# A fourth weight sum by an accumulating transfer, with some twenty steps in another order, in a fused pair of float32 transformer blocks

## The reference

```
gu = jnp.einsum('bsd,df->bsf', hn, w_gate_up[l])
act = jax.nn.silu(gu[..., :D_FF]) * gu[..., D_FF:]
h = h + jnp.einsum('bsf,fd->bsd', act, w_down[l])
```

## Time and profile before

| what | value |
|---|---|
| median of 3 runs | 1271.92 us (1271.25 to 1272.7) |
| the profiled execution | 1271.37 us, with a span of 1269.6 us |
| TensorE busy | 1253.5 us, 99% of the span |
| VectorE busy | 1042.7 us, 82% |
| ScalarE busy | 804.0 us, 63% |
| GpSimd busy | 192.4 us, 15% |
| read from HBM | 275.24 MB, 218 GB/s over the span |

### The profile page before, as it was taken

The page is one execution under the profiler, slowest core; times in us unless marked ns, Lnnn a source line. Parts: engine busy times, 40 slices in busy tenths (PEclk is TensorE's granted clock), DMA queues, the critical chain, the costliest instruction groups (busy, mean ns, idle before and its releaser), DMA issues.

```text
span 1269.6 us, 15538 instructions
## 1 busy us (share of the span) xinstructions
PE 1253.5 (99%) x5897; PEld 1028.9 (81%) x5897; DVE 1042.7 (82%) x1035; ACT 804.0 (63%) x986; POOL 192.4 (15%) x224
## 2 busy tenths in 40 slices
PE   9999999999999999999999999999999999999998
PEld 7888878888888878788778888788888877788886
DVE  6766689999799996767899997999977568999984
ACT  6674576665576664645766664766656466766662
POOL 6142130110001100102201101111001003301100
PEclk9999999999999999999999999999999999999999
DMA  9537498997649955568979978389745535999931
GB/s 333 174 100 231 133 313 254 268 270 248 201 151 255 269 168 180 188 226 215 320 249 245 271 251 255 116 237 274 219 166 173 184 125 168 315 286 262 266 135 44
DMA packets 143002, 277.32 MB, mean 218 GB/s; under 512 B 8992, under 2 KB 39896, under 8 KB 142928
## 3 DMA queue, kind: packets, MB, share of 16 engines
q1 hardware_dynamic: 120192, 229.67, 51.6%
q0 software_dynamic: 22288, 45.54, 19.7%
q10 hardware_dynamic: 448, 1.12, 0.2%
HBM read 275.24 MB, written 1.05 MB: 218 GB/s over the span
## 4 chain that ended last, share of the span: by engine, by line
PE 77%; DVE 12%; issue 4%; ACT 3%; DMA 3%; POOL 0%; DVEq 0%; SPq 0%; ACTq 0%
PE B L2102 14%; PE B L2104 14%; PE B L2103 14%; DVE w_lo L1359 7%; PE B L2558 6%; PE B L2560 6%; PE B L2559 6%; PE T L2102 3%; PE T L2104 3%; PE T L2103 3%; DMA VD<-in_ffn_w_gu 2%; DVE VD L1378 1%; DMA Z<-in_ffn_w_gu 1%; ACT w_hi L1082 1%; ACT w_hi L768 1%
## 5 line engine op out<-in xcount | busy, mean ns | idle before, releaser
L1359 DVE TENSOR_TENSOR w_lo<-w_raw,w_hi 128x2048 fp32r<-128x2048 f32 x129 | 296.5, 2299 | 87.5 <-ACT w_hi L768 87.2
L768 ACT ACTIVATE w_hi<-w_raw 128x2048 fp32r<-128x2048 f32 x129 | 247.1, 1918 | 102.7 <-PE B L2560 60.3
L2102 PE MATMUL B<-w_hi,xt_lo 128*128 128x512 f32 x652 | 260.5, 400 | 5.1 <-DVE w_lo L1359 2.1
L2104 PE MATMUL B<-w_hi,xt_hi 128*128 128x512 f32 x652 | 254.7, 391 | 0.0
L2103 PE MATMUL B<-w_lo,xt_hi 128*128 128x512 f32 x652 | 254.0, 390 | 0.0
L2558 PE MATMUL B<-w_hi,act_lo 128*128 128x512 f32 x440 | 172.5, 392 | 0.8 <-DVE w_lo L1359 0.4
L2560 PE MATMUL B<-w_hi,act_hi 128*128 128x512 f32 x440 | 171.4, 390 | 0.0
L2559 PE MATMUL B<-w_lo,act_hi 128*128 128x512 f32 x440 | 171.3, 389 | 0.0
L2102 PEld LDWEIGHTS B<-w_hi,xt_lo 128*128 128x128 f32 x652 | 122.4, 188 | 36.1 <-issue 6.2
L2104 PEld LDWEIGHTS B<-w_hi,xt_hi 128*128 128x128 f32 x652 | 122.4, 188 | 26.4
L2103 PEld LDWEIGHTS B<-w_lo,xt_hi 128*128 128x128 f32 x652 | 122.6, 188 | 23.3
(11 more groups left out here) (330 smaller groups left out, 2110.0 us busy)
## 6 DMA issues: line engine op xcount, KB each, us to landing
w_raw<-in_ffn_w_down SPq DMA_DIRECT2D x88, 512.0 KB, 5.8
Z<-in_ffn_w_gu SPq DMA_DIRECT2D x64, 512.0 KB, 8.1
w_raw<-in_ffn_w_gu SPq DMA_DIRECT2D x48, 512.0 KB, 5.2
nat<-in_ffn_w_gu SPq DMA_DIRECT2D x32, 512.0 KB, 7.8
QT<-in_ffn_w_gu SPq DMA_DIRECT2D x32, 512.0 KB, 7.0
Z<-in_ffn_w_gu POOLq DMA_DIRECT2D x32, 512.0 KB, 8.8
w_raw<-in_conv_w_in SPq DMA_DIRECT2D x24, 512.0 KB, 4.7
w_raw<-in_w_down SPq DMA_DIRECT2D x22, 512.0 KB, 6.6
```

The lines of the kernel that those rows point to most:

```text
L768: act.activation(whi[home(u)][:, :], raw[slot][:, :], ACT.Copy).then_inc(w_hi, 1)
L1359: dve.tensor_tensor(wlo[home(u)][:, :], src, whi[home(u)][:, :].bitcast(F32), ALU.subtract).then_inc(w_lo, 1)
L2102: pe.matmul(bank[:, :], lo[:, k, x], whi[s][:, c], start=first, stop=False, skip_group_check=more)
L2104: return pe.matmul(bank[:, :], hi[:, k, x], whi[s][:, c], start=False, stop=last, skip_group_check=more)
```

## The change

The changed kernel does the same arithmetic. Square 3 joins `ADDED_T4`: GpSimd issues one more accumulating transfer in each FFN, of B21 into VD, and VectorE's sum of it is gone. Besides, steps move in the lists of TensorE, VectorE and ScalarE; no matmul is added or removed. SyncE's list stays as it is.

```diff
--- before.py
+++ after.py
@@ -62,8 +62,8 @@
 OP = {name: i for i, name in enumerate(FFN_OPS)}
 FFN_UNITS = len(FFN_OPS)
 
-SUMS = ((1, "T1"), (1, "T2"), (2, "T1"), (2, "T2"), (3, "T1"), (3, "T2"), (3, "T4"))
-ADDED_T4 = (1, 2)
+SUMS = ((1, "T1"), (1, "T2"), (2, "T1"), (2, "T2"), (3, "T1"), (3, "T2"))
+ADDED_T4 = (1, 2, 3)
 
 
 def sums_of(f):
@@ -1120,11 +1120,11 @@
 
                 weights("N1b")
                 block("P1", 0)
+                act.wait_ge(rstd, 2 * ST[stat] + 2)
+                gate_of(0, u0 + OP["N0b", 0], PAIR[0] if f else F0)
                 act.wait_ge(sx_ok, f + 1)
                 act.wait_ge(w_used, u0 + OP["N0b", 0] + 1)
                 act.activation(yhi[:, :, :], xsum, ACT.Copy).then_inc(sx_hi, 1)
-                act.wait_ge(rstd, 2 * ST[stat] + 2)
-                gate_of(0, u0 + OP["N0b", 0], PAIR[0] if f else F0)
                 block("P2", 0)
                 gate_of(1, u0 + OP["N1b", 0], GU)
                 act_out(0)
@@ -1574,10 +1574,10 @@
             split_at(6)
             head_scale(1, Z[:, :, 512:1024], FOX_H, FOX_DH)
             mem_round_lo(0)
-            split_at(7)
             dve.wait_ge(c_hi, 1)
             low = slice(64, CK)
             dve.tensor_tensor(cT[low, :], B[3][low, 0:S], cT[low, :].bitcast(F32), ALU.subtract).then_inc(c_out, 1)
+            split_at(7)
             evac(EV_IN + 2, 5, Z[:, 1, 1536:2048], PAIR[2], "h0")
             heads_out(HT_KF, KT[:, 2:4, :], G_KF)
             split_at(8)
@@ -1737,13 +1737,17 @@
                     .then_inc(dve_step, 1)
                 return steps[0]
 
-            def x_sums(total):
+            def x_sums(total, second):
 
                 dve.wait_ge(dve_step, total)
                 a11, a12 = xsum[:, 0:4, 0:P], xsum[:, 4:8, 0:P]
                 a21, a22 = xsum[:, 0:4, P:S], xsum[:, 4:8, P:S]
-                link(dve.tensor_tensor(a22, a21, a22, ALU.subtract))
-                dve.tensor_tensor(a21, a11, a21, ALU.subtract)
+                if not second:
+                    steps[0] += 1
+                    dve.tensor_tensor(a22, a21, a22, ALU.subtract).then_inc(dve_step, 1)
+                    dve.wait_ge(dve_step, steps[0])
+                    dve.tensor_tensor(a21, a11, a21, ALU.subtract)
+                    return
                 link(dve.tensor_tensor(a11, a22, a11, ALU.subtract))
                 dve.tensor_tensor(a12, a12, a11, ALU.add).then_inc(sx_ok, 1)
 
@@ -1814,11 +1818,12 @@
                     hi, lo = act_parts(d)
                     dve.tensor_tensor(lo[:, :], act_bank(d)[:, :], hi[:, :].bitcast(F32), ALU.subtract).then_inc(act_lo, 1)
 
-                x_sums(total)
+                x_sums(total, False)
                 weights("N1b")
-                block("P1", 0)
+                x_sums(total, True)
                 dve.wait_ge(rstd, 2 * ST[stat] + 2)
                 act_of(0, PAIR[0] if f else F0)
+                block("P1", 0)
                 dve.wait_ge(sx_hi, f + 1)
                 dve.tensor_tensor(ylo[:, :, :], xsum, yhi[:, :, :].bitcast(F32), ALU.subtract).then_inc(sx_lo, 1)
                 block("P2", 0)
@@ -1827,11 +1832,11 @@
                 block("P5", 0)
                 block("P6", 0)
                 block("P3", 0)
-                weight_sum("T4", f, 0)
                 block("P7", 0)
                 weights("D0")
+                weight_sum("T4", f, 0)
+                result("C22", 0)
                 block("P4", 0)
-                result("C22", 0)
                 weights("D1")
                 result("C12", 0)
                 weight_sum("T1", f, 1)
@@ -1844,12 +1849,12 @@
                     square_act(p - 1, 0)
                     square_act(p - 1, 1)
                     block("P6", p)
-                    if p not in ADDED_T4:
-                        weight_sum("T4", f, p)
                     block("P3", p)
                     block("P7", p)
                     act_out(2 * p)
                     weights("Da", p - 1)
+                    if p not in ADDED_T4:
+                        weight_sum("T4", f, p)
                     act_out(2 * p + 1)
                     block("P2", p)
                     result("C22", p)
@@ -1876,9 +1881,10 @@
                 act_out(FJ - 1)
                 if kv:
                     kv_round_lo(1)
+                if kv:
+                    kv_round_lo(2)
                 split_at(u0 + FFN_UNITS)
                 if kv:
-                    kv_round_lo(2)
                     kv_round_lo(3)
                 split_at(u0 + FFN_UNITS + 1)
 
@@ -1933,9 +1939,9 @@
             conv_gate(1)
             conv_evac(4)
             split_at(U_COUT, U_COUT + 1)
-            conv_taps(2)
             conv_lo(0)
             conv_lo(1)
+            conv_taps(2)
             conv_evac(5)
             conv_taps(3)
             conv_gate(2)
@@ -2058,8 +2064,8 @@
             combine(4)
             diff_max(11)
             o_sum(1)
+            o_norm(1)
             heads_lo(0)
-            o_norm(1)
             diff_max(12)
             evac(EV_V1, U_V1 + 1, VD[:, 1, HALF:D], PAIR[1], "h6")
             combine(5)
@@ -2547,11 +2553,11 @@
                                       not first)
                     ins.then_inc(w_used, 1)
 
-                def down_part(d, u, t, half):
+                def down_part(d, u, t, half, k0=0, k1=2):
 
                     hi, lo = act_parts(d)
                     slot = home(u)
-                    for k in range(2):
+                    for k in range(k0, k1):
                         c = slice(k * D + half * HALF, k * D + half * HALF + HALF)
                         x = slice((2 * k + t) * P, (2 * k + t) * P + P)
                         o = PAIR[half][t][:, :]
@@ -2632,22 +2638,35 @@
                 turn_act(FJ - 1, GROUPS - 1)
                 if kv:
                     kv_round(1)
-                down("Db", SQUARES - 1, (lambda: kv_round(2)) if kv else (lambda: None))
+                d, u = down_ready("Db", SQUARES - 1)
+                down_part(d, u, 0, 0)
+                down_part(d, u, 0, 1)
+                if kv:
+                    kv_round(2)
+                down_part(d, u, 1, 0)
+                d1, u1 = down_ready("DN2", 0)
+                down_part(d1, u1, 0, 0).then_inc(tok0_done, 1)
                 if kv:
                     kv_round(3)
-                d, u = down_ready("DN2", 0)
-                down_part(d, u, 0, 0).then_inc(tok0_done, 1)
-                down_part(d, u, 0, 1).then_inc(tok0_done, 1)
-                down_part(d, u, 1, 0).then_inc(tok1_half, 1)
-                if nxt:
+                down_part(d1, u1, 0, 1).then_inc(tok0_done, 1)
+                down_part(d, u, 1, 1).then_inc(w_used, 1)
+                down_part(d1, u1, 1, 0).then_inc(tok1_half, 1)
+                if f == 0:
                     for j in range(4):
                         turn(nxt, 0, j, h, h_waits(nxt))
-                down_part(d, u, 1, 1).then_inc(w_used, 1)
+                down_part(d1, u1, 1, 1, 0, 1)
+                if f and nxt:
+                    turn(nxt, 0, 0, h, h_waits(nxt))
+                    turn(nxt, 0, 1, h, h_waits(nxt))
+                down_part(d1, u1, 1, 1, 1, 2).then_inc(w_used, 1)
+                if f and nxt:
+                    turn(nxt, 0, 2, h, h_waits(nxt))
+                    turn(nxt, 0, 3, h, h_waits(nxt))
 
             ffn(0, "ffn0", h_waits("ffn0"), nxt="ffn1")
-            ffn(1, "ffn1", h_waits("ffn1"), turned=True)
-
-            first_group(U_CIN, "cin", PAIR[0], h, h_waits("cin"))
+            ffn(1, "ffn1", h_waits("ffn1"), turned=True, nxt="cin")
+
+            first_group(U_CIN, "cin", PAIR[0], h, h_waits("cin"), turned=True)
             def conv_feed(p, is_b):
 
                 if not is_b:
@@ -2696,9 +2715,9 @@
                 if k < 2:
                     conv_feed(k + 2, True)
             last_group(U_COUT + 2, PAIR[1], "ffn2")
-            ffn(2, "ffn2", h_waits("ffn2"), turned=True)
-
-            ffn(3, "ffn3", h_waits("ffn3"), kv=True)
+            ffn(2, "ffn2", h_waits("ffn2"), turned=True, nxt="ffn3")
+
+            ffn(3, "ffn3", h_waits("ffn3"), kv=True, turned=True)
 
             def q_round(j):
 
@@ -2866,18 +2885,24 @@
             pe.wait_ge(w_lo, U_O + 2)
             for k in (4, 5):
                 out_heads(1, k, 0)
+            out_heads(0, 4, 1)
             heads_pair(3)
-            for k in (4, 5):
+            out_heads(0, 5, 1)
+            out_heads(1, 4, 1)
+            pe.wait_ge(ao_lo, 4)
+            for half in range(2):
+                for k in (6, 7):
+                    out_heads(half, k, 0)
+            for k in (6, 7):
                 out_heads(0, k, 1)
-            pe.wait_ge(ao_lo, 4)
-            for t in range(TOKS):
-                for k in (6, 7):
-                    out_heads(0, k, t)
-            for k in (6, 7):
-                out_heads(1, k, 0)
-            for k in range(4, KD):
+            for k in (5, 6):
                 out_heads(1, k, 1)
```

(7 more changed lines are left out.)

## The result

The changed kernel takes 1293.12 us in the median of 5 runs (1292.91 to 1294.24), the kernel before 1271.76 (1271.25 to 1272.7) beside it: the ratio is 1.017, with a 95% interval of 1.0157 to 1.0184. It is slower, as forecast, but by 21.4 us instead of 7, outside the range. The profiled execution has a span of 1291.1 us against 1269.6.

The account below looks back on a forecast made before the run. The prediction took TensorE, 99% busy at full clock, as the bound, so only its waits could change. It set 16.0 us lost against 8.9 won, +7.1, and predicted 1279.0 us, range 1269.5 to 1285.

Parts of the forecast that it names:

- the chain in square 0: VectorE's T4 behind P7 and D0 delays ScalarE's copy of P4, then act_out(1); D1 on TensorE starts 3.0 us later.
- the sum of square 0: Five FFNs: 3.0 us lost in four, 2.5 in FFN 2, plus 0.3 each for B12's load; 16.0 us lost.
- my bound from above: B12's load in square 0, at 6.6 us or slightly more, lands at 843.9, delaying T1 by up to 1.0 us.
- T4 of square 3: Its sum goes from VectorE to a covered transfer, so P3's wait in square 3 goes; 1.9 us won.
- The x_sums in halves: At N1b, the low part comes 1.3 us earlier and its waits go; 2.5 us won in all.
- The turns at the FFN's tails: Turning for the next stage is covered by other matmuls; 0.7 us each from FFNs 1 and 2, 0.55 ahead of FFN 4.
- The small moves: Reorderings at the cumulated sum, conv_lo, a kv round and the differential attention's output projection; together 2.5 us won.
- the cover that I had called over a microsecond: Behind N1b's delayed half, the token sums' low part and P2 have over a microsecond in hand; costed at nothing.
- The first: Rival: square 0's new chain is covered, D1 starts less than 1.8 us later, kernel faster, 1261; chance 0.15.
- The second: Rival: B12's load meets the down weights, T1 waits 1 to 1.5 us in each FFN; 1283 to 1286, chance 0.12.
- The third: Rival: the won parts aren't won, turning in halves makes tile 1's h late; 1281 to 1283, chance 0.10.
- the fourth: Rival: square 3's accumulating transfer is late, costing 1.1 us in each FFN; 1284 to 1285, chance 0.04.
- the fifth: Rival: the new wait is half as large and the signs cancel; within 0.2% of 1272, chance 0.07.

Follow-up runs that it names:

- b12_first: The changed kernel with SyncE's load of B12 ahead of that of B21 in square 0; 1284.76 us, ratio 1.0109 to the kernel before.
- filler12: The changed kernel with twelve further matmuls, read by nobody, ahead of D1 in square 0 of each FFN; 1284.94 us, ratio 1.0108 to the kernel before.
- sq0_back: The changed kernel with VectorE's list in square 0 put back, all other edits kept; 1263.6 us against 1270.76 for the kernel before, ratio 0.9944.
- t4_three_alone: The kernel before with one edit alone, T4 of square 3 by an accumulating transfer; 1269.33 us against 1271.53, ratio 0.9982.
- sq0_back_again: The changed kernel with VectorE's list in square 0 put back, run once more in the third group; 1264.42 us against 1271.19, ratio 0.9948.
- actout_first: The changed kernel with act_out(1) ahead of the sum of T1 on VectorE; 1291.26 us, ratio 1.0162 to the kernel before.
- t4_split_b12: The changed kernel with square 0 put back, T4 in two halves around P7, and B12's load ahead of B21's; 1265.34 us, ratio 0.9954 to the kernel before.

## Why the prediction was right or wrong

**The direction was right, and so was the chain in square 0.** Set to P7's start, T4 should end at 835.9 in the clock of the earlier trace rows, ScalarE's copy of P4 at 837.8, D1's subtraction at 842.35. Measured, and moved back by 11.29 us (P7 starts at 842.74 now and would have started at 831.45 there): 835.86, 837.82 and 842.34.

**The step that failed is the sum of square 0, "4 x 3.0 + 2.5 + 5 x 0.3 = 16.0 us lost"; it measured some 29.** Two things are wrong in it.

The smaller: the waits. From P7's start to D1's take 15.34, 15.40, 15.49, 15.37 and 15.65 us now, against 10.99, 11.00, 11.41, 10.97 and 10.98; less P7's 0.4 won that is 19.9 us instead of 16.0. It is B12's load that I mis-sized: T1 waits 0.81, 0.88, 0.96, 0.84 and 1.12 us for it, and `b12_first` put it at 5.0 us of TensorE's waits in all. Its issue was right (836.8 forecast, 836.86 found). The landing was my bound from above (843.9 forecast, 843.78 found), and I had taken 0.3 us for each FFN where the row behind that bound, the 6.6 us of the earlier trace rows, gave about 1. It was the nearest row: a load behind another in the same queue. The 4.4 of the earlier trace rows belonged to the first of three loads issued together. The fit of the Trainium skill ("DMA: Bandwidth & Descriptors", Anatomy of one DMA) gave 842.7 here; that section states it for transfers that GpSimd issues, and these are SyncE's. The run shows 1.1 us more, and the measurement decides. FFN 2, which I had discounted by 0.5, lost 3.7 against 4.0 to 4.3 in the others.

The larger: a term that is missing altogether, the clock, 9.8 us. I read that the clock was full in all slices and priced a wait of TensorE at its length, though I forecast one of 3.4 us in each FFN, where the longest in the kernel before was 0.9 us: no row could show what follows so long a wait. Behind all five, matmuls run at 1.2 GHz. `filler12` shows that the standing still is the cause: the feeding engines and the transfers do what they did, and the slow matmuls are gone. The Trainium skill says it plainly ("TensorE: Matmul & The Clock Gate", HAM oscillation): idle stretches of TensorE take the clock down, and what comes next pays. It also gives 426.7 ns for 512 columns at the lower level (Wait — 56ns, not 53.3ns?), and the rows here have 0.43 us. By that rule there should have been a rival: the forecast with a half clock behind each of five waits. With the two losses as measured, 19.9 + 9.8 against 8.9 won, it would have been 1292.7.

**The won terms, 8.9 forecast, measured 7** (7.2 and 6.8 in two groups). By the starts in the traces of the kernel before and of `sq0_back`: T4 of square 3 won 2.0 (1.9 forecast; 2.2 by the times of `t4_three_alone`). The x_sums in halves won 1.5 (2.5): N1b's waits are gone, but 0.44 and 0.23 us stand now at P2 in FFNs 0 and 4, the cover that I had called over a microsecond. The turns at the FFN's tails won 0.8 each after FFNs 1 and 2 (0.7 forecast), and ahead of FFN 4 nothing: one wait of 0.81 us at the first turn took the place of three of together 0.80. The small moves won about 1.9 (2.5): the kv round 0.7, the cumulated sum 0.5, the conv step only 0.2, since the wait moved to the feed behind it, and 0.5 in the output projection. These are 7.0 us. The two traces are 9.3 us apart; the rest is in waits that come and go between executions of one kernel, at the down products behind square 0 and at D1 of FFN 2: `sq0_back_again`, the same kernel, has 0.77 and 0.81 us at two down products of FFN 1 where `sq0_back` has none.

**The rivals.** The first, that D1 is covered, fell: it waits in all FFNs. The second, B12's load later than reckoned, was true in its mechanism (T1's wait is just under its 1 to 1.5 us in four FFNs and 1.12 in FFN 4, over the 1 us that the prediction named as a sign of being wrong) but not large enough alone. The third was not seen as such, though the won terms are 2 us smaller; the fourth fell (`t4_three_alone`); the fifth fell. What carries most of the error stood in none of them. The prediction gives the forecast's own range once as 1276 to 1281 and once as 1275 to 1282; the measured time lies above both.

## What to carry to other kernels

When a forecast puts a wait of several microseconds on TensorE, price what follows it too: here a wait of 3.8 us cost 5.7 on average, since 5 to 12 matmuls behind it ran at half the clock. Add up the time in which the feeding engine will have nothing to do: in FFN 3 VectorE's four holes, 4.0 us, are what D1 came later. A move on a feeding engine is to be followed through each queue that waits for it: an operation that a copy on another engine needs, and after which the first engine has little else to do, costs what of the copy it can't fill (1.39 us at P4), and a load whose issue is conditioned on it holds back every load behind it in the same list. And where each product of an engine is awaited in turn, as VectorE's in square 0, reordering moves a wait without removing it (`actout_first`, `t4_split_b12`), while taking work off the engine, as the transfer of T4 did, wins time. Where something else had time in hand, as at N1b and at the tails, the reorderings of this change did win, some 5 us in all.

## What the runs showed that I had not expected

Sixty idle-time matmuls whose result nobody reads made the kernel faster, 1284.94 against 1293.12 us. The half clock is not a sharp function of the wait alone: of two waits of 2.76 us ahead of D1 in one execution of `b12_first`, in FFNs 0 and 1, one was followed by six matmuls at 0.43 and the other by none; what distinguishes them no run here shows. And the number of slow matmuls behind waits of almost equal length (3.66, 3.73, 3.83, 3.70, 3.97 us) was 5, 12, 8, 5 and 11. The granted clock shows only that it came back 2.8, 5.6, 4.6, 3.0 and 5.4 us behind D1's start; why so differently stays open too.
